# Prompt attention: turning exponential rows by a product with a diagonal of inverse sums

## The reference

```
for blk in range(L // Q_BLOCK):                     # 512 // 128 = 4
    s = (q_nope . k_nope + q_pe . k_pe) * scale      # keys 0 to q1, so 128, 256, 384 or 512
    p = softmax(where(pos_q >= pos_k, s, -inf))
    out[blk] = p . v[:, :q1]
```

## Time and profile before

| what | value |
|---|---|
| three runs | 1614.13, 1618.27 and 1617.96 us; median 1617.96 |
| the profiled execution | 1621.41 us, of which the span of the trace is 1619.8 |
| busy: PE, PEld, DVE, ACT, POOL | 94%, 88%, 48%, 37%, 23% of the span |
| the loop over pairs of heads | from 83.6 to 328.5 us after the start of the span |

### The profile page before, as it was taken

One profiled execution on the slowest core, in us unless ns is written; L12 is line 12 of the kernel. 1 busy time (PEld: TensorE's weight loads), 2 busy tenths in 40 slices (PEclk: granted clock), 3 DMA queues, 4 the chain that ended last, 5 costly groups with the idle time before them and its releaser, 6 DMA issues.

```text
span 1619.8 us, 32125 instructions
## 1 busy us (share of the span) xinstructions
PE 1515.4 (94%) x11453; PEld 1425.9 (88%) x11453; DVE 771.9 (48%) x1227; ACT 603.9 (37%) x1085; POOL 366.7 (23%) x430
## 2 busy tenths in 40 slices
PE   5989988889999899999999999789999999999995
PEld 5966666668988899999999999689999999999994
DVE  3866546545554454343244454964443522344332
ACT  6344454475654233321133233342333311233221
POOL 0286665434421102210022133020012200122000
PEclk9989899889999999999999999899999999999997
DMA  7123323323323222222222465512222222222211
GB/s 175 24 60 83 85 83 88 104 87 112 95 86 121 63 81 78 87 82 79 81 86 78 137 187 160 199 31 81 78 79 80 82 88 87 79 78 83 83 57 59
DMA packets 245279, 147.57 MB, mean 91 GB/s; under 512 B 42071, under 2 KB 239614, under 8 KB 244190
## 3 DMA queue, kind: packets, MB, share of 16 engines
q1 hardware_dynamic: 238114, 139.39, 29.4%
q0 software_dynamic: 6704, 7.20, 1.7%
q10 hardware_dynamic: 396, 0.13, 0.0%
HBM read 128.42 MB, written 18.26 MB: 91 GB/s over the span
## 4 chain that ended last, share of the span: by engine, by line
PE 86%; DVE 6%; ACT 3%; issue 2%; DMA 1%; POOL 1%; SPq 0%; ACTq 0%; DVEq 0%; POOLq 0%
PE bank L861 60%; PE bank L781 7%; PE bank L1103 3%; PE bank L976 3%; PE bank L1068 3%; PE bank L924 3%; PE bank L941 2%; PE bank L990 1%; PE bank L984 1%; ACT arena L1358 1%; DVE tmpa L2315 1%; DVE arena L2020 1%; DVE arena L2342 1%; DVE sq L2315 1%; PE bank L1009 1%
## 5 line engine op out<-in xcount | busy, mean ns | idle before, releaser
L861 PE MATMUL bank<-arena_parts,wR 128*128 128x288 f32 x4224 | 567.1, 296 | 6.0 <-ACT arena_parts L1435 3.7
L861 PEld LDWEIGHTS bank<-arena_parts,wR 128*128 128x128 f32 x4224 | 563.2, 188 | 7.8 <-issue 5.9
L861 PE MATMUL bank<-side_parts,wR 128*128 128x288 f32 x3360 | 447.3, 295 | 1.1 <-DVE tmpa L2387 1.1
L861 PEld LDWEIGHTS bank<-side_parts,wR 128*128 128x128 f32 x3360 | 445.5, 188 | 1.5 <-issue 1.3
L1841 DVE TENSOR_TENSOR wR<-wraw,wR 128x1024 fp32r<-128x1024 f32 x159 | 232.8, 1464 | 238.1 <-ACT wR L1421 236.6
L744 POOL TENSOR_TENSOR arena_parts<-sq,arena_parts 128x576 f32 x64 | 91.7, 1433 | 674.4 <-ACT arena_parts L1654 674.4
L1421 ACT ACTIVATE wR<-wraw 128x1024 fp32r<-128x1024 f32 x159 | 167.2, 1052 | 201.9 <-PE bank L861 187.4
L1358 ACT ACTIVATE arena<-bank 128x256 f32<-128x256 f32 (+9 forms) x223 | 96.1, 446 | 151.7 <-PE bank L984 53.0
L1651 ACT ACTIVATE tmpa<-bank 128x576 f32<-128x576 f32 x64 | 41.8, 653 | 195.3 <-PE bank L861 195.3
L2238 DVE TENSOR_TENSOR sq<-tmpa 128x576 f32<-128x576 f32 x64 | 48.5, 758 | 127.0 <-ACT tmpa L1651 127.0
L781 PE MATMUL bank<-ident,arena 128*128 128x128 f32 (+4 forms) x400 | 70.7, 299 | 20.0 <-DVE arena L2020 15.9
(11 more groups left out here) (301 smaller groups left out, 1622.3 us busy)
## 6 DMA issues: line engine op xcount, KB each, us to landing
wraw<-in_mlp_w SPq DMA_DIRECT2D x128, 512.0 KB, 3.9
side<-in_cache_ckv SPq DMA_DIRECT2D x128, 128.0 KB, 2.1
wraw<-in_ssm_w_glu SPq DMA_DIRECT2D x16, 512.0 KB, 3.9
s_state_to_out<-side SPq DMA_DIRECT2D x16, 256.0 KB, 2.5
s_in_to_state<-yblk SPq DMA_DIRECT2D x8, 512.0 KB, 2.6
s_in_to_out<-side SPq DMA_DIRECT2D x64, 64.0 KB
wraw<-in_mla_w_o SPq DMA_DIRECT2D x8, 512.0 KB, 4.5
side<-s_in_to_state SPq DMA_DIRECT2D x2, 2048.0 KB, 13.0
```

What stands on the lines that cost most here:

```text
L861: return pe.matmul(bank[:, a, 0:HALF], wR[:, s, wp, k, :], tokens(k, xp)[:, a * HALF:(a + 1) * HALF], start=(first and j == 0), stop=(last ...
```

## The change

The exponential is written to the SBUF buffer `probs` instead of back into the score bank, so ScalarE first waits until the turn of the unit three before has read that buffer. VectorE no longer multiplies the rows. It multiplies the 128x128 identity by the inverse sums and so makes a diagonal matrix, one of three in `inverse_sums`, which lies in a buffer (`sq`) that this loop did not use. TensorE turns a tile by an ordinary float32 product of the tile with that diagonal, which scales it too, where it used its transpose form with the identity. `p_sb` now tells that the diagonal is there; its number and its waiters are unchanged. The order of the instructions on each engine stays as it was.

```diff
@@ -202,6 +202,7 @@
         hid = sq
+        inverse_sums = sq.rearrange("p a n -> p (a n)")[:, 0:3 * P].rearrange("p (c n) -> p c n", c=3)
         scaled = kpR[:, :]
@@ -929,7 +930,8 @@
                 pe.wait_ge(p_sb, p * 8 + (u + 1 + CREDIT))
                 for t in range(blk + 1):
-                    ins = transpose(bank23[:, u % 2, t * P:(t + 1) * P], probs[u % 3][:, t * P:(t + 1) * P])
+                    ins = pe.matmul(bank23[:, u % 2, t * P:(t + 1) * P], probs[u % 3][:, t * P:(t + 1) * P],
+                                    inverse_sums[:, u % 3, :], start=True, stop=True)
                 ins.then_inc(t_done, 1)
@@ -1484,7 +1486,8 @@
                 act.wait_ge(nm_ready, p * 8 + (u + 1))
-                act.activation(score_banks[u % 3][:, 0:n], score_banks[u % 3][:, 0:n], ACT.Exp,
+                act.wait_ge(t_done, p * 8 + (before(u, 3) + CREDIT))
+                act.activation(probs[u % 3][:, 0:n], score_banks[u % 3][:, 0:n], ACT.Exp,
                                bias=stat[:, u % 3:u % 3 + 1],
                                accum_out=stat[:, 3 + u % 3:4 + u % 3]).then_inc(p_exp, 1)
@@ -2017,7 +2020,7 @@
                 own(dve.reciprocal(stat[:, 32 + c:33 + c], stat[:, 3 + c:4 + c]))
                 settle()
-                dve.tensor_scalar(probs[c][:, 0:n], score_banks[c][:, 0:n], stat[:, 32 + c:33 + c], None, ALU.mult)\
+                dve.tensor_scalar(inverse_sums[:, c, :], ident[:, :], stat[:, 32 + c:33 + c], None, ALU.mult)\
                     .then_inc(p_sb, 1)
```

## The result

The changed kernel takes 1633.4 us (median; 1628.19 to 1640.65) where the kernel before takes 1617.78 in the same series: a ratio of 1.0095, 95% interval 1.0066 to 1.0125. In a second series it was 1631.45 against 1617.71, ratio 1.0076 (1.0056 to 1.0096). So it's slower by 14 to 16 us, more than the 4.9 us that can be told from no change, and above my range (1608 to 1629).

A forecast was written before the change was run, and what follows sets the result against it. TensorE bounds the kernel (86% of the chain). Loop: 8 x (27.69 + 1.04 + 0.45) + 2.74 for the first pair + 10.1 for three falls = 246.2 against 244.87 us, +1.4; forecast 1619 us, range 1608 to 1629.

The forecast's parts named there:

- The undisturbed pair: Head pair without a clock fall: 27.69 us before, plus 1.04 for the chain and 0.45 for waits on GpSimd.
- GpSimd's share: Part of TensorE's wait before unit 6's turn, from the diagonal waiting for GpSimd's operation: 0 to 1.1 us, taken as 0.45.
- my sum: One pair's chain at full clock, followed through TensorE's waits for units 0, 2 and 6: 1.04 us longer.
- the port's 0.45: Unit 6's diagonal waits for GpSimd at the shared SBUF port: 0.45 us a pair, out of 0 to 1.1.
- half of 2.2: Second records of a pair's 20 tiles add 2.2 us on TensorE at full clock; half of it is covered.
- VectorE's saving: Diagonal instead of scaled copy saves 0.07 to 0.47 us a unit; nearly all given back in the pair.
- The diagonals: Duration of each diagonal on VectorE: 0.28 us where GpSimd is idle, up to 1.4 beside it.
- the first pair's slower start: First of the eight pairs: 2.74 us (33.34 - 30.60) longer than the others, carried over unchanged.
- The falls of the clock: TensorE's clock drops in the loop's pairs: three expected after the change, at 3.35 us each, 10.1 in all.
- The slower rival: Every pair falls: seven or eight clock falls in the loop at 3.35 us each, 1633 to 1636 us; chance 0.12.

The follow-up runs named there:

- the first profile: Profiled execution of the changed kernel in its first series, 1628.19 us, the shortest of its four; four of eight pairs undisturbed.
- the filled kernels: Three float32 identity products put ahead of unit 0's turn in each pair, in both kernels: changed kernel 1618.55 us, kernel before 1603.51 us.
- the second profile: Changed kernel run again unchanged: 1631.45 us; seven of eight pairs had a stretch at half clock.
- the kernel with the record alone: Kernel before with its turn made a plain float32 product with the identity, scaled copy kept: 1646.12 us.
- the filling products: Three plain float32 products of the identity with itself ahead of unit 0's turn, overwritten by it; in the kernel before 1603.51 us, 0.991 of the unfilled one.
- ScalarE's diagonals: Changed kernel with each diagonal made by ScalarE behind its unit's exponential, VectorE keeping the reciprocal: 1634.36 us.
- the kernel with one record a tile: Changed kernel with exponentials and diagonals in the type for which TensorE takes one record a product: 1629.62 us unfilled, 1612.76 with three identity products ahead of unit 0's turn.
- the run with transposes as filling: Kernel before with six identity transposes (0.66 us) ahead of unit 0's turn: 1604.2 us, 0.9916 of the kernel before.

## Why the prediction was wrong

*The undisturbed pair* came out close, 29.18 forecast and 29.34 measured, but in part by luck. Two records a tile are in the rows, and so is the wait before unit 6's turn, 0.77 us, where I had about 0.5 and GpSimd's share. But my sum let unit 5's tiles lie in that wait and had no step that hangs on ScalarE's exponentials. One does. ScalarE copies unit 5's turned rows, takes the exponential of unit 7 and makes four more copies without a pause, and the products of line 962 (964 after the change) need the last of these. Unit 5's copy before the change, in the pair from 239.29:

```profile
261.23 0.49 ACT L1358 ACTIVATE arena<-bank 128x384 f32<-128x384 f32 x1 [0.22 <-PE bank L781]
```

After it, in the pair from 242.22, the same copy, the last copies and the products:

```profile
265.33 0.49 ACT L1360 ACTIVATE arena<-bank 128x384 f32<-128x384 f32 x1 [0.61 <-PE bank L933]
...
267.33 0.64 ACT L1360 ACTIVATE arena<-arena 64x128 f32 x2
...
268.11 0.65 PE L964 MATMUL bank<-side,arena 128*32 128x128 f32 x16
```

From the pair's start unit 5's copy comes at 21.94 us before and 23.11 after, and the products at 24.75 and 25.89, 1.14 later; unit 7's turn adds 0.50, and that is the pair's 1.65. ScalarE is done at 267.97 and TensorE, with the values behind unit 6's turn, at 268.02: the two paths end together, which is why a shorter wait for GpSimd gained nothing. Without the port's 0.45 my sum was 1.04; that term stood in for a path that I had left out. The added records were worth 1.4 to 1.94 us net rather than half of 2.2, and VectorE's saving 0.3 to 0.4 at the most.

*The diagonals* took 0.28 to 0.29 us beside an idle GpSimd and up to 1.30 beside a busy one, as forecast; at unit 6 0.59 to 0.60 in the first profile's undisturbed pairs. My term of 0.45 a pair was too high for later pairs, where removing the wait gains nothing, and it left out the first: there unit 0's diagonal met GpSimd's work (VectorE's diagonal, then TensorE's turn in that pair):

```profile
99.94 1.30 DVE L2023 TENSOR_SCALAR sq<-ident,stat 128x128 f32<-128x128 f32 x1
```

```profile
101.29 0.79 PE L933 MATMUL bank<-sq,arena 128*128 128x128 f32 x2 [1.63 <-DVE sq L2023]
```

I had taken the first pair's slower start over as it was, 2.74 us. In the filled kernels it is 33.25 - 29.34 = 3.91 after, 30.61 - 27.83 = 2.78 before: 1.1 us more.

*The falls of the clock* are the step that failed. I let them shrink from 7 x 2.91 = 20.4 us to 3 x 3.35 = 10.1, a gain of 10.3 that made +11.9 of the pairs into +1.4. I argued that the stretch before a fall gets 0.22 us more work. That reason failed. TensorE still idles 0.61 us there for the diagonal of unit 0. The stretches before and in a fall of the changed kernel, and the same place of its undisturbed pair:

```profile
161.60:165.00 3.40, 2.79 (x20) 2.15 (x20) 2.44 (x11) 1.23 (x5) 0.00 (x0) 1.00 0.59 148
165.00:168.42 3.42, 3.42 (x13) 2.26 (x12) 1.45 (x5) 2.51 (x11) 0.00 (x0) 0.50 0.36 90
...
252.60:256.00 3.40, 2.78 (x19) 2.00 (x17) 2.34 (x10) 1.40 (x5) 0.00 (x0) 1.00 0.56 138
```

The same work (2.79 and 2.78 us of 3.40) and the same wait ended in a fall once and not the other time; what decides between the two isn't shown. Each fall was indeed of another length, 3.4 us (1.6 us lost) or 10.2 (4.8 lost), where it was 6.8 (2.9 lost); but over the executions the loss stayed, 14.2 us before and 12.9 after. Without that gain my own terms give 11.9 + 1.1 = 13.0 for the loop, against 13.3 measured in the filled kernels; that they agree so well is the same luck with the port's term. The 2 to 3 us behind the loop are the part with no cause shown.

The slower rival had the time (1633 to 1636), and in the second profile also its seven falls, but not their price: 3.35 us each by its sum, where five took about 1.5 and one 4.8. The first profile had four. As much was lost to falls as before, not more. Its shape, one long fall in each pair, did come in the kernel with the record alone.

The kernel before with the filling products is faster than both: 1603.51 us.

## What to carry to other kernels

An instruction's second record on the engine that sets the end was paid nearly in full; work taken from an engine that is mostly waited for by a few instructions gains little unless those few move. Follow each added piece of work through every engine that waits for it: here unit 5's added records moved ScalarE's copies, and these the pair's end. Do not credit a change with fewer falls of the clock for a little more work ahead of them; fill the wait that they follow on both sides, and compare then. Such filling was worth 14 us to the kernel before and 13 to the changed one, about as much as the change lost; in a kernel with shorter pairs falls came at another place in spite of it.

## What the runs showed of the hardware

Six records of filling work (0.66 us) in one wait of each pair brought the granted clock of the loop from 0.92 to 0.99. The wait alone is not enough for a fall (0.73 us with ScalarE's diagonals, and six pairs at 1.00), and filling it is not always enough to prevent one (the kernel with one record a tile). The Trainium skill ("TensorE: Matmul & The Clock Gate", Part 4, "PE-mode transpose") says that the full clock doesn't engage for the transpose form; the run with transposes as filling doesn't agree here, with six of seven later pairs at 1.00 and 1604.2 us against 1603.5 with products. And slowing a kernel by the record alone made its falls longer, 10.2 us in every pair from the second on where they had been 6.8, so that 2.2 us of added work in a pair cost 29 us in all (1646.12 against 1616.8 of the kernel before in that series) rather than 18.
